# ScalarE makes the code products of the routing stage, and the first two blocks' rows are cleared, indexed and gathered in it

## The reference

```python
row_tok = jnp.zeros((prows,), jnp.int32).at[dest].set(flat_tok[order])
row_g = jnp.zeros((prows,), h.dtype).at[dest].set(flat_g[order])
xs = xt[row_tok].reshape(nb, MOE_BLOCK, d)
hid = jax.nn.silu(xb @ w_e_gate[e]) * (xb @ w_e_up[e])     # for each block, e its expert
ys = hid @ w_e_down[e]
y = jnp.zeros_like(xt).at[row_tok].add(ys.reshape(prows, d) * row_g[:, None])
```

## Time and profile before

| | |
|---|---|
| median of three runs | 2310.2 us (2307.55 to 2312.79) |
| the profiled execution's own time | 2311.14 us |
| its span, first to last instruction | 2309.5 us |
| TensorE matmuls busy | 2109.7 us, 91% of the span |
| VectorE busy | 1665.3 us, 72% |
| ScalarE busy | 1489.6 us, 64% |
| GpSimd busy | 487.9 us, 21% |
| mean granted clock of TensorE | 0.963 of full speed |

### The profile page before, as it was taken

The page is one execution under the profiler, slowest core; times in us unless marked ns, Lnnn a source line. Parts: engine busy times, 40 slices in busy tenths (PEclk is TensorE's granted clock), DMA queues, the critical chain, the costliest instruction groups (busy, mean ns, idle before and its releaser), DMA issues. The chain is left out here.

```text
span 2309.5 us, 35723 instructions
## 1 busy us (share of the span) xinstructions
PE 2109.7 (91%) x11088; PEld 1747.1 (76%) x11088; DVE 1665.3 (72%) x3111; ACT 1489.6 (64%) x2272; POOL 487.9 (21%) x562
## 2 busy tenths in 40 slices
PE   6999999978889999999899957999999999999970
PEld 6798989755578888888788846878888888888860
DVE  5323332167588888888544578989999999999977
ACT  5323241277588888887544425878888887888867
POOL 0112111135123333331100001222222222222221
PEclk9999999979989999999999978999999999999985
DMA  6535352543442222222344328998688789998838
GB/s 210 169 134 184 122 184 97 154 102 95 106 106 72 73 72 72 72 63 92 100 153 154 137 86 313 374 316 266 211 297 277 219 271 364 326 308 287 264 73 309
DMA packets 223181, 420.65 MB, mean 182 GB/s; under 512 B 50504, under 2 KB 99736, under 8 KB 221912
## 3 DMA queue, kind: packets, MB, share of 16 engines
q1 hardware_dynamic: 190512, 316.48, 40.9%
q0 software_dynamic: 31520, 101.49, 15.3%
q10 hardware_dynamic: 1040, 1.31, 0.2%
HBM read 437.68 MB, written 86.39 MB: 227 GB/s over the span
## 5 line engine op out<-in xcount | busy, mean ns | idle before, releaser
L2763 DVE TENSOR_TENSOR moe_w_lo<-fetch_w_raw,moe_w_hi 128x1024 fp32r<-128x1024 f32 x376 | 435.3, 1217 | 13.5 <-ACT moe_w_hi L2692 13.3
L2692 ACT ACTIVATE moe_w_hi<-fetch_w_raw 128x1024 fp32r<-128x1024 f32 x376 | 368.8, 1052 | 71.6 <-DMA fetch_w_raw<-in_w_e_up_dram 36.2
L2817 PE MATMUL moe_ps_gu<-moe_w_hi,moe_xT_hi 128*128 128x512 f32 x736 | 292.4, 397 | 4.4 <-DVE moe_xT_lo L2774 4.4
L2819 PE MATMUL moe_ps_gu<-moe_w_hi,moe_xT_lo 128*128 128x512 f32 x736 | 288.4, 392 | 0.0
L2818 PE MATMUL moe_ps_gu<-moe_w_lo,moe_xT_hi 128*128 128x512 f32 x736 | 288.4, 392 | 0.0
L1634 DVE TENSOR_TENSOR fox_p_lo<-fox_ps_t,fox_p_hi 128x512 fp32r<-128x512 f32 (+4 forms) x352 | 211.0, 610 | 42.8 <-ACT fox_p_hi L1568 42.5
L1568 ACT ACTIVATE fox_p_hi<-fox_ps_t 128x512 fp32r<-128x512 f32 (+4 forms) x352 | 181.8, 535 | 68.4 <-PE fox_ps_t L1709 67.6
L2769 DVE TENSOR_TENSOR moe_d_lo<-fetch_d_raw,moe_d_hi 128x1024 fp32r<-128x1024 f32 x184 | 213.1, 1220 | 10.9 <-ACT moe_d_hi L2700 9.3
L1709 PE MATMUL fox_ps_t<-ident,fox_s 128*128 128x128 f32 (+1 forms) x1216 | 195.7, 275 | 13.3 <-ACT fox_s L1561 13.1
L1621 DVE CUSTOM_DVE_ANT_0 fox_s<-fox_ps_r,fox_ncum 128x512 f32<-128x512 f32 (+4 forms) x352 | 193.4, 566 | 14.0 <-PE fox_ps_r L1692 8.7
L512 ACT ACTIVATE proj_qk_out<-proj_ps_chunk 128x512 f32<-128x512 f32 x52 | 31.1, 598 | 252.9 <-PE proj_ps_chunk L746 252.9
(11 more groups left out here) (373 smaller groups left out, 5156.6 us busy)
## 6 DMA issues: line engine op xcount, KB each, us to landing
fetch_w_raw<-in_w_e_gate_dram SPq DMA_DIRECT2D x192, 512.0 KB
fetch_w_raw<-in_w_e_up_dram SPq DMA_DIRECT2D x192, 512.0 KB
fetch_d_raw<-in_w_e_down_dram SPq DMA_DIRECT2D x92, 1024.0 KB
ahead_raw<-in_w_in_dram SPq DMA_DIRECT2D x24, 1024.0 KB, 5.3
gates_wide<-in_x_dram SPq DMA_DIRECT2D x16, 512.0 KB
h<-gates_wide POOLq DMA_DIRECT2D x16, 512.0 KB, 3.3
gates_wide<-qT SPq DMA_DIRECT2D x32, 256.0 KB, 4.5
mix_h<-h SPq DMA_DIRECT2D x16, 512.0 KB, 3.7
```

Of the source, the lines that this page charges most:

```text
L2692: nc.scalar.activation(w_hi[:, k], w_raw[:, k].rearrange("p j n -> p (j n)"), ACT.Copy).then_inc(gu_high, 1)
L2763: nc.vector.tensor_tensor(w_lo[:, k], w_raw[:, k].rearrange("p j n -> p (j n)"), w_hi[:, k].bitcast(F32), ALU.subtract).then_inc(gu_split, 1)
L2817: nc.tensor.matmul(out, xT_hi[:, slot, k], w_hi[:, k, cols], start=k == 0, stop=False)
L2819: done = nc.tensor.matmul(out, xT_lo[:, slot, k], w_hi[:, k, cols], start=False, stop=k == KT - 1)
```

## The change

- ScalarE gets a program in the routing stage. It first clears both slots of `x` (a copy of `lane` times 0, twice 128x1024), then makes the code products, one column at a time: 32 activations of 128x64 with the column's code as scale. Each adds one to `code_carried`.
- VectorE makes `at_block` first, then `at_lane`, then the gate product, and no code product. TensorE waits for both counts at each part.
- Behind `tokens` VectorE writes the indices of blocks 0 and 1, ahead of the last three decoding steps. GpSimd, behind its constants, waits for each clearing and index and issues the gathers of blocks 0 and 1 in the routing stage. `x`, `index` and the gathers' semaphores move to the space that outlives it.
- The expert stage loses the two clearings, two index copies and two gathers. Its counts start two blocks later.

```diff
+            for b in range(2):
+                pool.wait_ge(emptied, b + 1)
+                pool.wait_ge(indexed, b + 1)
+                wait(pool, touched, b)
+                nc.gpsimd.tensor_tensor(tick[:, b:b + 1], still[:], still[:], ALU.add).then_inc(touched, 1)
+                pool.indirect_dma_start(out=fetch["x"][:, b], out_offset=None, in_=t["h1"],
+                                        in_offset=bass.IndirectOffsetOnAxis(ap=fetch["index"][b][:], axis=0),
+                                        bounds_check=SEQ - 1, oob_is_err=False).then_inc(fetch["x_in"][b], 16)
+
+        @block.scalar
+        def _(act):
+            act.wait_ge(consts, 5)
+            for b in range(2):
+                nc.scalar.activation(fetch["x"][:, b].rearrange("p (a n) -> p a n", n=P),
+                                     lane[:].unsqueeze(1).to_broadcast([P, D // P, P]), ACT.Copy, scale=0.0).then_inc(emptied, 1)
+            for part in range(4):
+                act.wait_ge(placed, part + 1)
+                for n in range(part * T // 2, (part + 1) * T // 2):
+                    nc.scalar.activation(carried[:, n, 0], at_block[:, n], ACT.Copy, scale=code[:, n:n + 1]).then_inc(code_carried, 1)
...
+                v.tensor_tensor(at_block[:, cols], spread(block_f, ROWS),
+                                number[:].unsqueeze(1).to_broadcast([P, T // 2, ROWS]), ALU.is_equal).then_inc(placed, 1)
                 v.tensor_tensor(at_lane[:, cols], spread(lane_f, P), lane[:].unsqueeze(1).to_broadcast([P, T // 2, P]),
                                 ALU.is_equal)
-                then(v.tensor_tensor(at_block[:, cols], spread(block_f, ROWS),
-                                     number[:].unsqueeze(1).to_broadcast([P, T // 2, ROWS]), ALU.is_equal))
+                dve.wait_ge(placed, part + 1)
                 v.tensor_tensor(carried[:, cols, 1], at_block[:, cols],
...
-                v.tensor_tensor(carried[:, cols, 0], at_block[:, cols], spread(code, ROWS), ALU.mult).then_inc(carried_ready, 1)
+                                .unsqueeze(2).to_broadcast([P, T // 2, ROWS]), ALU.mult).then_inc(gate_carried, 1)
...
+            for b in range(2):
+                v.tensor_scalar(fetch["index"][b][:], route["tokens"][:, b:b + 1], 0.0, None, ALU.add).then_inc(indexed, 1)
...
-                    pe.wait_ge(carried_ready, n // (T // 2) + 1)
+                    pe.wait_ge(gate_carried, n // (T // 2) + 1)
+                    pe.wait_ge(code_carried, n + T // 2)
...
-            nc.gpsimd.memset(x[:, 0], 0.0).then_inc(cleared, 1)
-            pool.wait_ge(cleared, 2)
-            gather(0, 0, 0)
-            nc.gpsimd.memset(x[:, 1], 0.0).then_inc(cleared, 1)
-            pool.wait_ge(cleared, 3)
-            gather(1, 1, 0)
+            pool.wait_ge(cleared, 1)
...
-            pick_index(0, 0, 0)
-            pick_index(1, 1, 0)
```

More of the change, by code:

```diff
@@ L2421, in phase_route @@
         carried = m.sb("carried", [P, 2 * T, WHAT, ROWS])
+        tick = m.sb("tick", [1, 2])
+        still = m.sb("still", [1, 1])
         ps_rows = m.ps("ps_rows", [P, 512])
@@ L2425, in phase_route @@
         step = m.sem("step")
-        carried_ready = m.sem("carried_ready")
+        placed = m.sem("placed")
+        gate_carried = m.sem("gate_carried")
+        code_carried = m.sem("code_carried")
+        emptied = m.sem("emptied")
+        indexed = m.sem("indexed")
+        touched = m.sem("touched")
         inverted = m.sem("inverted")
@@ L2462, in _ @@
                                     allow_small_or_imprecise_dtypes=True))
+            constant(nc.gpsimd.memset(still[:], 0.0))
+            for b in range(2):
[16 more added lines that the diff above has]
+                    nc.scalar.activation(carried[:, n, 0], at_block[:, n], ACT.Copy, scale=code[:, n:n + 1]).then_inc(code_carried, 1)
         @block.vector
@@ L2480, in spread @@
                     return ap[:, cols].unsqueeze(2).to_broadcast([P, T // 2, n])
+                v.tensor_tensor(at_block[:, cols], spread(block_f, ROWS),
+                                number[:].unsqueeze(1).to_broadcast([P, T // 2, ROWS]), ALU.is_equal).then_inc(placed, 1)
                 v.tensor_tensor(at_lane[:, cols], spread(lane_f, P), lane[:].unsqueeze(1).to_broadcast([P, T // 2, P]),
                                 ALU.is_equal)
-                then(v.tensor_tensor(at_block[:, cols], spread(block_f, ROWS),
-                                     number[:].unsqueeze(1).to_broadcast([P, T // 2, ROWS]), ALU.is_equal))
+                dve.wait_ge(placed, part + 1)
                 v.tensor_tensor(carried[:, cols, 1], at_block[:, cols],
                                 route["gate"][part // 2][:, part % 2 * T // 2:(part % 2 + 1) * T // 2]
-                                .unsqueeze(2).to_broadcast([P, T // 2, ROWS]), ALU.mult)
-                v.tensor_tensor(carried[:, cols, 0], at_block[:, cols], spread(code, ROWS), ALU.mult).then_inc(carried_ready, 1)
+                                .unsqueeze(2).to_broadcast([P, T // 2, ROWS]), ALU.mult).then_inc(gate_carried, 1)
             dve.wait_ge(inverted, 1)
@@ L2527, in phase_experts @@
         d_lo = m.sb("d_lo", [P, DT, D], F32R)
-        index = [m.sb(f"index{i}", [P, 1], I32) for i in range(2)]
+        index, x, x_in = fetch["index"], fetch["x"], fetch["x_in"]
         code = [m.sb(f"code{i}", [P, 1], I32) for i in range(2)]
@@ L2532, in phase_experts @@
         still = m.sb("still", [1, 1])
-        x = m.sb("x", [P, 2, D])
         xT_hi = m.sb("xT_hi", [P, 2, KT, P], F32R)
@@ L2557, in phase_experts @@
         gated = m.sem("gated")
-        x_in = [m.pool_dma_sem(f"x_in{i}") for i in range(2)]
         x_turned = m.sem("x_turned")
@@ L2640, in gather @@
             def gather(b, slot, use):
-                pool.wait_ge(indexed, b + 1)
+                pool.wait_ge(indexed, b - 1)
                 wait(pool, x_turned, b - 1)
-                touch(0, gathering, b)
+                touch(0, gathering, b - 2)
                 pool.indirect_dma_start(out=x[:, slot], out_offset=None, in_=t["h1"],
@@ L3009, in hybrid_block_kernel @@
             fetch = {"w_raw": raw.sb("w_raw", [P, KT, 2, D_EXPERT]), "d_raw": raw.sb("d_raw", [P, DT, D]),
+                     "x": raw.sb("x", [P, 2, D]), "index": [raw.sb(f"index{i}", [P, 1], I32) for i in range(2)],
+                     "x_in": [raw.pool_dma_sem(f"x_in{i}") for i in range(2)],
                      "gu_in": [raw.sem(f"gu_in{i}") for i in range(4)], "dn_in": [raw.sem(f"dn_in{i}") for i in range(2)]}
```

## The result

| | before | after |
|---|---|---|
| median of the runs | 2309.0 us (6 runs, 2306.9 to 2312.8) | 2316.9 us (6 runs, 2314.7 to 2319.9) |
| ratio | | 1.0028, 95% interval 1.0018 to 1.0038 |
| profiled execution: span, mean granted clock | 2309.5 us, 0.963 | 2318.3 us, 0.961 |
| first VectorE instruction of the routing stage | 1379.53 | 1380.97 |
| opening of the expert stage | 1396.35 | 1404.03 |

The changed kernel is slower by about 0.3%: outside the forecast range, and on the other side of it.

What follows compares the result with a forecast made beforehand. TensorE, busy 91% of the span, bounds the kernel; the change touches only a hole before block 0's first gate/up product. That starts 1.7 us earlier, taking the 2310.2 us median to 2308.5; range 2305.3 to 2311.5.

Steps and rivals of the forecast that it cites:

- VectorE's code products leave: Routing stage, VectorE: a part takes 2.36 us in place of 3.07 without the four code products.
- ScalarE's products: Routing stage, ScalarE: 32 code products of 128x64, 0.25 us apart, 2.0 us a part.
- rival B: Routing stage: ScalarE becomes the bound at 0.33 us a product; 2309.4 us; chance 0.15.
- TensorE's 64 passes: Routing stage: TensorE itself becomes the bound, its passes end at 1393.3, 0.7 us gained.
- The sum's 0.12 a pass: Routing stage, TensorE: after 22 passes until 1388.2, the other 42 take 0.12 us each.
- The two issues: Routing stage, GpSimd: issuing the two gathers takes 1.05 us each, short because VectorE is idle then.
- Rival C: Expert stage: the loads give the shift back, TensorE's stalls from 1412 to 1540 grow; 2310.2 us; chance 0.17.
- Two indices and two gathers move in front of the stage's end: Routing stage's end: GpSimd arrives last, so the expert stage opens at 1398.8, 2.4 us later than before.
- rival D: Routing stage's end waits until the gathers have landed; gate/up at 1410.8 to 1413.5, 2313.5 to 2316.2 us; chance 0.09.
- The row against D: Steady state, GpSimd: the tick at 1445.76 follows directly behind an issue, with no idle time before it.
- From there the stage is taken to run as before, only shifted: Expert stage from block 0's first gate/up product: the rest runs unchanged, so only that product's 1.7 us earlier start counts.

Runs made afterwards that it cites:

- e3: Changed kernel with 64 unused bytes ahead of the expert stage's four weight tiles and 64 behind; ratio to before 1.0011, 2311.9 us.
- p4: Kernel before with 160 unused bytes behind the expert stage's weight tiles; 2324.2 us.
- s2: Kernel before with 64 unused bytes behind the expert stage's weight tiles only; 2322.2 us.
- d1: The early probe: kernel before with one more GpSimd gather in the routing stage, issued 14 us before the stage's end; 2308.4 us.
- d2: The late probe: kernel before with one more GpSimd gather, issued when TensorE has ended the route passes; 2312.6 us.
- m2: Changed kernel, weight tiles at a multiple-of-256 distance, ticks and gathers back in the expert stage, 32-byte pad in the mixing stage; ratio 0.9976, 2304.1 us.
- e4: Changed kernel with 64 unused bytes ahead of and behind the weight tiles, ticks and gathers moved back into the expert stage; ratio 1.0004.

## Why the prediction was wrong

**What held.** *VectorE's code products leave*: 2.36 us a part was forecast, 2.35 measured (1380.97 to 1383.32). *ScalarE's products*: 0.25 apart, measured 0.245, and rival B is out. *TensorE's 64 passes*: it became the bound, and the clock decided; the gain was 1.5 us where 0.7 was the middle value and 1.6 the best end. The sum's 0.12 a pass was near: in the changed kernel 15 passes took 3.13 us at a clock of 0.50, 0.21 each, and 51 took 5.74 us at 1.00, 0.11 each. *The two issues*: 1.12 and 1.04 long, where 1.05 was taken. But the first took 1.12 with VectorE idle (it had ended at 1395.46), as long as the issue of before that the prediction sets beside a remainder, so these rows show no price of a remainder. Rival C is out too: from 1460 to 1550 ScalarE waited 15.4 us for loads, against 16.3 in the earlier trace rows.

**The step that failed first** is in "Two indices and two gathers move in front of the stage's end": "now the expert stage opens 0.94 us behind VectorE", "then as long behind GpSimd, at 1398.8". The 0.94 us belongs to VectorE, whose drain took 17 ns. GpSimd's, with two gathers out, took 6.36; from the end of the second issue (1398.40) to the opening it was 5.6 us and not 0.94. That was rival D, with the right mechanism and nearly the right price: from opening to gate/up 6.9 us were measured where it has 7.0, and from the second issue to the end of the drain 5.3 (1397.36 to 1402.7) where it has 6.1 to 8.8; the opening, forecast for +24.3 to +27.0, came at +23.1. It got 0.09. Its text sets one row against it, GpSimd's tick behind an issue, and for it stands only "I see no stage that ends on a transfer that the program doesn't itself wait for", so the stage ends could say nothing either way. The trace of before has the row elsewhere: near the end of the expert stage the code drains GpSimd itself between its last two scatters (L2676). The issue of the first of them, and that drain:

```profile
2232.69 1.55 POOL L2655 DMA_INDIRECT acc<-moe_y,moe_code  x1 [0.58 <-issue]
```

```profile
L2676 POOLq DRAIN  x1: 6517/6517/6517, 2232.5 to 2232.5; - x1
```

6.5 us with a scatter just issued, against 0.05 at the routing stage's end, where nothing was out. The scatter landed at 2238.89 and the drain ended at 2238.98. The row against D, GpSimd's next tick directly behind an issue, speaks of an issue, not of a drain; those are different waits.

**The step that failed for more** is the frame of the whole sum: "From there the stage is taken to run as before, only shifted". Only rival C doubted it, over the loads, and no term had the products themselves. Of the loss of 7.8 us some 6 lie there, 3312 products 1.9 ns longer each, since the change put 8256 bytes ahead of one operand of every product and left the other where it was. D alone, at the 2.0 us that it cost at the first product, would have been 2311.0, just inside the range's upper end of 2311.5; e3, which has it alone, measured 2311.9, just outside. With both it came to 2316.9.

The range has a slip of its own: half the spread of the runs (2307.55 to 2312.79) is 2.6 us and the prediction added 1.3, so by its own words it would go from 2304.0 to 2312.8. The result lies outside that too.

That the place of a tile costs time is measured: with only xT moved by 64 bytes, gate/up products took 233.3 ns in place of 227.2. What in the hardware makes it so, no run here shows.

## What to carry to other kernels

When a change adds or moves a tile in SBUF, compare the addresses of every later product's moving and stationary tile before and after, and keep their distance a multiple of 256 bytes; here that was worth 1.9 to 6 ns a product, and a 32-byte pad in a stage that nobody had meant to touch gave 0.16%. Don't let GpSimd issue a gather shortly before the end of a stage: the stage's end then waits for the transfer, so an early gather hides nothing unless it is out 6 to 9 us before the other engines are done (it landed after 6.0 us in the late probe, and after 8.8 in the early one, beside loads). Before saying that the rest "runs as before, only shifted", count the matmuls in a window where TensorE is always busy.

## What the runs showed of the hardware

- In these layouts the time of a 512-column fp32r product behind another went by how the moving and the stationary tile lie to each other modulo 256 bytes: 227.2 to 227.9 ns at a distance of 0, 229.1 at 192, 233.0 to 233.4 at 32, 64, 128, 160 and 224 (the last in the mixing stage of the kernel before). It is not symmetric (233.2 to 233.3 at 64, 229.1 at 192). At 32, 160 and 224 the stationary tile also lies off a multiple of 64, and no run separates the two. A distance of 96 wasn't tried.
- A mean can hide an uneven split: in p4 the gate/up products of w_hi with xT_hi came 237.2 ns before their successor and the two other kinds 231.3 and 231.4, while in s2 all three kinds had 233.2 to 233.5, with nearly the same mean. Why isn't known.
- GpSimd's DRAIN took 0.05 us with nothing out, 6.0 to 6.5 with gathers or a scatter just issued, and 9.2 with a gather that landed after 8.8. It ended 0.1 us behind the last landing in each of five cases (the scatter of before, after, e3, d1, d2).
- The same 64 passes took 8.9 us (after, e3, m2) or 10.3 (e4): the granted clock rose from 0.50 to 1.00 3.1 to 3.2 us after work began, or only 6.1.
